# Expert tokens gathered in slots of 64 and two experts side by side in TensorE's array, in a two-layer trunk step

## The reference

```python
hf = rms_norm(x, p['norm_ffn_w']) * (1.0 + sc_f) + sh_f
x = x + g_f * hier_moe(hf, p)

def hier_moe(h, p):
    ...
    gw, gsel = lax.top_k(gp, 1)
    ...
    tw, ti = lax.top_k(jax.nn.softmax(el, axis=-1), TOP_K)
    tw = tw / jnp.sum(tw, axis=-1, keepdims=True)
    eid = gsel * EXPERTS_PER_GROUP + ti
    combine = jnp.sum(jax.nn.one_hot(eid, N_EXPERTS, dtype=jnp.float32) * (gw * tw)[..., None], axis=1)
    hg = jnp.einsum('nd,edf->nef', x, p['moe_w_gate'])
    hu = jnp.einsum('nd,edf->nef', x, p['moe_w_up'])
    act = jax.nn.silu(hg) * hu * combine.astype(x.dtype)[..., None]
    y = jnp.einsum('nef,efd->nd', act, p['moe_w_down'])
```

## Time and profile before

| | |
|---|---|
| median of 3 runs | 1421.93 us |
| span of the profiled execution | 1411.4 us |
| between the span and the median | 10.5 us |
| PE (matmul) busy | 1236.9 us, 88% |
| PEld (weight load) busy | 968.0 us, 69% |
| VectorE (DVE) busy | 678.2 us, 48% |
| ScalarE (ACT) busy | 491.7 us, 35% |
| GpSimd (POOL) busy | 86.5 us, 6% |
| DMA | 299.0 MB, mean 212 GB/s |
| expert loads | 64 of 3072 KB, median 10.1 us from issue to landing |

### The profile page before, as it was taken

How to read it: one execution, slowest core, us unless ns; L and a number is a source line. 1 busy time by engine, 2 the same in 40 slices (tenths; PEclk the granted TensorE clock), 3 DMA queues, 4 the chain that set the end, 5 groups by cost and what they waited for, 6 DMA issues and landing times.

```text
span 1411.4 us, 18228 instructions
## 1 busy us (share of the span) xinstructions
PE 1236.9 (88%) x7508; PEld 968.0 (69%) x7508; DVE 678.2 (48%) x857; ACT 491.7 (35%) x550; POOL 86.5 (6%) x93
## 2 busy tenths in 40 slices
PE   4689678998679999999967996798886999999997
PEld 3489568797656666666664985687776666666665
DVE  0255535443355556656423654445424556566652
ACT  2234521112244444444213444111322544444440
POOL 0000203130000000000000011222100000000000
PEclk8799879999789999999988997899996999999999
DMA  9744600121508888888865354102060488888960
GB/s 389 337 179 179 242 9 31 35 90 44 225 0 336 338 338 339 346 345 336 343 269 244 146 199 172 34 31 94 1 243 26 179 345 335 335 340 344 354 268 32
DMA packets 15195, 299.00 MB, mean 212 GB/s; under 512 B 1920, under 2 KB 1920, under 8 KB 2176
## 3 DMA queue, kind: packets, MB, share of 16 engines
q1 hardware_dynamic: 14688, 296.67, 53.5%
q0 software_dynamic: 416, 1.05, 0.2%
HBM read 295.61 MB, written 2.10 MB: 211 GB/s over the span
## 4 chain that ended last, share of the span: by engine, by line
PE 79%; DVE 6%; issue 5%; ACT 5%; DMA 3%; POOL 1%; SPq 0%; DVEq 0%; POOLq 0%; ACTq 0%
PE ps L824 16%; PE ps L795 8%; PE ps L796 8%; PE ps L797 8%; PE ps L713 4%; PE ps L483 3%; PE ps L485 3%; PE ps L484 3%; PE ps L663 3%; PE ps L638 3%; PE ps L659 3%; DMA param<-in_param 3%; PE ps L459 2%; PE ps L838 1%; PE ps L862 1%
## 5 line engine op out<-in xcount | busy, mean ns | idle before, releaser
L1602 DVE TENSOR_TENSOR ring_r<-ring,arena_r 128x2048 fp32r<-128x2048 f32 x124 | 284.3, 2292 | 129.5 <-ACT arena_r L1127 129.5
L1127 ACT ACTIVATE arena_r<-ring 128x2048 fp32r<-128x2048 f32 x124 | 236.7, 1909 | 231.2 <-PE ps L797 231.2
L795 PE MATMUL ps<-arena_r 128*128 128x512 f32 x512 | 231.3, 452 | 5.4 <-DVE ring_r L1602 3.5
L824 PE MATMUL ps<-ring,arena 128*128 128x512 f32 x512 | 230.3, 592 | 1.0 <-DVE arena L1608 1.0
L797 PE MATMUL ps<-ring_r,arena_r 128*128 128x512 f32 x512 | 202.5, 395 | 0.0
L796 PE MATMUL ps<-arena_r 128*128 128x512 f32 x512 | 202.3, 395 | 0.0
L824 PEld LDWEIGHTS ps<-ring,arena 128*128 128x128 f32 x512 | 96.8, 189 | 99.0 <-issue 91.9
L795 PEld LDWEIGHTS ps<-arena_r 128*128 128x128 f32 x512 | 96.3, 188 | 38.9 <-issue 16.7
L483 PE MATMUL ps<-arena_r 128*128 128x256 f32 x384 | 109.7, 286 | 10.4 <-DVE ring_r L1256 10.4
L796 PEld LDWEIGHTS ps<-arena_r 128*128 128x128 f32 x512 | 96.6, 189 | 31.8 <-issue 14.4
L797 PEld LDWEIGHTS ps<-ring_r,arena_r 128*128 128x128 f32 x512 | 96.0, 188 | 22.6
(11 more groups left out here) (301 smaller groups left out, 1548.9 us busy)
## 6 DMA issues: line engine op xcount, KB each, us to landing
ring<-in_moe SPq DMA_DIRECT2D x64, 3072.0 KB, 10.1
ring<-in_ada_w SPq DMA_DIRECT2D x16, 3072.0 KB, 11.1
ring<-in_w_feat SPq DMA_DIRECT2D x8, 3072.0 KB, 14.1
ring<-in_w_tok SPq DMA_DIRECT2D x2, 2112.0 KB, 24.0
ring<-in_w_out SPq DMA_DIRECT2D x2, 2048.0 KB, 7.3
ring<-in_w_out SPq DMA_DIRECT2D x4, 1024.0 KB, 4.9
param<-in_param SPq DMA_DIRECT2D x2, 1501.5 KB, 23.4
const<-in_const SPq DMA_DIRECT2D x1, 1899.0 KB, 16.6
```

The source lines that it names most:

```text
L795: mm(out, x_hi, hi[:, k], start=k == 0, stop=False)
L824: done = mm(bank(4 + half), act_t[:, i % 2, kk * P:(kk + 1) * P], ring[i % RING][:, at:at + 512], start=i == 0 and kk == 0, stop=i == PER_ ...
L1127: go(w_hi[:, 0:4096].rearrange("p (w n) -> p w n", w=2)[:, :, cols], ring[j][:, 0:4096].rearrange("p (w n) -> p w n", w=2)[:, :, cols], AC ...
L1602: tt(low_w, raw_w, high_w, ALU.subtract).then_inc(sem[name], 1)
```

## The change

The gather becomes one by expert, with 64 slots (`CAP`) for each, and the experts are worked in 16 pairs.

- Path: the condition is now `fullest < CAP + 1`, no expert with more than 64 tokens. The rank of a token is counted per expert instead of per group (`mask32`, five products of 32 columns instead of 4).
- Selection (`select`): an equality with the slot number, 8 experts x 64 slots = 512 columns, for one group at a time, in two buffers.
- Gather: for one group at a time, again 8 x 4 products of 512 columns. Group 0 is gathered ahead; of the next group two feature tiles are gathered in each pair. The gathered tokens `xg` are plain float32, copied alternately by ScalarE and VectorE, not split.
- Gate/up (L816) and down (L863): full precision, weights not split, so L1127, L1602 and their waits are gone from this path. The first expert of a pair takes columns 0 to 63 of the array (and PSUM partitions 0 to 63), the second columns 64 to 127, by `tile_position`; the instructions of the two alternate. Gate/up of a pair is 16 products of 512 columns, down 8.
- The slot weights are made pair by pair (four products of 2 columns, L807), the `sel` transposes too (two per pair, L849, beside the two of the activations, L851).
- After every pair its 128 rows are written out as high and low part and scattered (L827, 16 products of 256 columns), summed in PSUM banks 4 to 7 over all pairs. The residual comes after the last, all 16 instructions in one go.
- Loads: two transfers per expert, gate/up (2048 KB, waits for `up_mm`, the gate/up products of four experts earlier) and down (1024 KB, waits for `down_mm`).
- The first expert's split, which stood beside the output projection, moves into the dense path.

```diff
+CAP = HD
+PAIRS, TURN = N_EXPERTS // 2, PER_GROUP // 2
+GU_W = 4096
...
-                for e in range(RING):
-                    slot_free(l, HEAD_SLOTS - RING + e)
-                    ring_in(e, (src["moe"][l, e], SLOT))
-                with sp.Fori(1, N_EXPERTS // RING) as turn:
...
+                for q in range(PAIRS):
+                    for half in range(2):
+                        for e in (2 * q, 2 * q + 1):
+                            if e < RING:
+                                if half == 0:
+                                    slot_free(l, HEAD_SLOTS - RING + e)
+                            else:
+                                name = "down_mm" if half else "up_mm"
+                                sp.wait_ge(sem[name], rise(l, name, e - RING + 1))
+                            if half == 0:
+                                sp.dma_start(ring[e % RING][:, 0:GU_W], src["moe"][l, e][:, 0:GU_W]).then_inc(slot_in[e % RING], 16)
+                            else:
+                                sp.dma_start(ring[e % RING][:, GU_W:SLOT], src["moe"][l, e][:, GU_W:SLOT]).then_inc(down_in[e % RING], 16)
...
+                def gate_up(q):
...
+                    for k in range(KT):
+                        for i in range(2):
+                            last = mm(ps[64 * i:64 * i + 64, q % 2, :].rearrange("p (w n) -> p w n", w=2),
+                                      xg[:, g % 2, k, c0 + 64 * i:c0 + 64 * i + 64], weights[i][:, k],
+                                      start=k == 0, stop=k == KT - 1, tile_position=(0, 64 * i), skip_group_check=True)
+                    last.then_inc(sem["up_mm"], 2)
...
+                def pair_step(q):
...
+                    gate_up(q)
+                    if q > 0:
+                        scatter(q - 1)
+                    if g < N_GROUPS - 1:
+                        pe.wait_ge(sem["sel"], rise(l, "sel", g + 2))
+                        for n in range(2):
+                            gather(g + 1, 2 * turn + n, 2 + n)
+                    pe.wait_ge(sem["g_act"], rise(l, "g_act", q + 1))
+                    for s in range(NS):
+                        nc.tensor.transpose(ps[:, q % 2, TOK + s * P:TOK + (s + 1) * P], sel[:, g % 2, s, c0:c0 + P], ident)
+                    for kk in range(2):
+                        last = nc.tensor.transpose(ps[:, q % 2, kk * P:(kk + 1) * P], gat[:, q % 2, kk * P:(kk + 1) * P], ident)
+                    last.then_inc(sem["tr_mm"], 1)
...
+                    pe.wait_ge(sem["act_t"], rise(l, "act_t", q + 1))
...
+                    for half in range(2):
                         for kk in range(2):
...
+                                last = mm(ps[64 * i:64 * i + 64, 2 + half, :], act_t[:, q % 2, kk * P + 64 * i:kk * P + 64 * i + 64],
+                                          ring[(2 * q + i) % RING][:, at:at + 512], start=kk == 0, stop=kk == 1,
+                                          tile_position=(0, 64 * i), skip_group_check=True)
+                    last.then_inc(sem["down_mm"], 2)
+                    if q < PAIRS - 1:
+                        pe.wait_ge(sem["st_dve"], rise(l, "st_dve", q + 1))
+                        slot_weights(q + 1, q % 2)
```

More of the change, by code:

```diff
@@ L785, in step @@
                         down(e, j, last)
[L787 to L809, removed]
-                        for kk in range(2):
[L811 to L826, removed]
@@ new lines, in landed, with gather @@
+                def landed(arrived, e, per_layer, before):
+                    j = e % RING
+                    pe.wait_ge(arrived[j], l * (16 * per_layer) + 16 * (before + e // RING + 1))
+                def gather(g, k, bank_out):
+                    for n, (x, s) in enumerate((x, s) for s in range(NS) for x in (ht_hi, ht_lo)):
+                        last = mm(bank(bank_out), x[:, s, k * P:(k + 1) * P], sel_r[:, g % 2, s, :], start=n == 0, stop=n == 3)
+                    last.then_inc(sem["ga_mm"], 1)
@@ new lines, in scatter @@
+                def scatter(q):
+                    pe.wait_ge(sem["y_lo"], rise(l, "y_lo", q + 1))
+                    pe.wait_ge(sem["st_dve"], rise(l, "st_dve", q + 1))
+                    for f in range(KT):
+                        for y in (y_hi, y_lo):
+                            last = mm(ps[:, 4 + f // 2, (f % 2) * TOK:(f % 2 + 1) * TOK], y[:, f * P:(f + 1) * P], sel_t[:, q % 2, :],
+                                      start=q == 0 and f % 2 == 0 and y is y_hi, stop=q == PAIRS - 1 and y is y_lo, skip_group_check=True)
+                    last.then_inc(sem["scatter_mm"], 1)
@@ L866, in _ @@
-                    for name, n in (("cb_mm", 16), ("gate_mm", 32), ("up_mm", 32)):
+                            name = "ga_dve" if k % 2 else "ga_act"
+                            pe.wait_ge(sem[name], rise(l, name, (k - 4) // 2 + 1))
+                        gather(0, k, k % 4)
+                    pe.wait_ge(sem["c_lo"], rise(l, "c_lo", 1))
+                    slot_weights(0, 7)
+                    for q in range(PAIRS):
+                        pair_step(q)
+                    scatter(PAIRS - 1)
@@ L867, in _ @@
+                    for name, n in (("cb_mm", 16), ("gate_mm", 32)):
                         pe.sem_inc(sem[name], n)
@@ L1475, in _, with residual @@
                 tt(hT[:, 0:2, :].rearrange("p m t -> p (m t)"), gn, zg, ALU.mult).then_inc(sem["gn_out"], 1)
-                def residual(gate, tiles):
+                def residual(gate, tiles, bank0=0):
                     for f in tiles:
```

279 lines of the change are left out of this document (134 added, 145 removed).

## The result

| | before | after |
|---|---|---|
| median | 1421.53 us (1420.16 to 1423.93, 4 runs) | 1307.28 us (1306.3 to 1311.93, 4 runs) |
| ratio | | 0.921, 95% interval 0.918 to 0.924 |
| span of the profiled execution | 1411.4 us | 1305.4 us |

The change is faster by 7.9%. The forecast was 1309.0 us, between 1291 and 1345.

The account below looks back on a forecast made before the run. The prediction took TensorE to bound the kernel. Savings of 51.1 (pairs), 2.9 (entry) and 2.4 us (exit) per layer, 112.8 for both, cut the span from 1411.4 to 1298.6; adding 10.5 gave 1309 us, range 1291 to 1345.

Parts of the forecast that it names:

- What bounds it: While the experts run, TensorE sets the pace, busy 100%; taking away the weight split gains nothing by itself.
- Two tiles at 2.0 times: In gate/up and down, two column tiles run side by side at 2.0 times, with the products issued interleaved.
- The terms of a pair: TensorE's pieces for two experts sum to 16.12 us, or 14.04 without a gather; 51.1 us less per layer.
- The first pair: First two experts of a layer: no scatter covers the silu and its table load, so 14.93 us.
- Entry and exit: Gather start to first expert product 10.5 us, 2.9 less; last down projection to layer end 10.5 us, 2.4 less.
- Next layer: Change to layer two: adaLN loads and parameters come later, about 9.5 us after layer end; zero, up to 3 us lost.
- DMA: Expert weight loads: 6.29 MB per pair take 15.0 us at 420 GB/s, so DMA does not set the pace.
- the rival: Among the experts, DMA sets the pace below 381 GB/s; 1355 us at 346 GB/s, 1337 at 358; chance 0.20.
- The sum: Both layers: 56.4 us less each, 112.8 in all; span 1298.6 us, plus 10.5 from span to median, 1309 us.

Follow-up runs that it names:

- e3: The changed kernel with half the columns of every expert transfer, so half the bytes: 1306.97 us.
- e4: The changed kernel with the scatter moved behind the transposes and expert transfers of half the columns: 1286.46 us in one execution.
- e8: The changed kernel with scatter and slot-weight products moved before the down projection, and expert transfers of half the columns: 1274.51 us in one execution.
- e1: The changed kernel with one tile's products all issued before the other's instead of alternating: 1478.3 us in one execution.
- e7: The changed kernel with the scatter behind the transposes and the slot-weight products moved between scatter and down projection: 1272.32 us, ratio to before 0.897.
- e2: The changed kernel with the scatter of the pair before moved into the wait before the down projection: 1281.09 us, ratio to before 0.904.
- e0: The kernel before, unchanged, run again with each execution's time beside its span: 1420.29 us, median of ten executions.
- e5: The changed kernel with one 3 MB transfer per expert, waiting for the down projection four experts earlier: 1343.75 us, ratio to before 0.948.

## Why the prediction was right, and where it was not

**What bounds it.** Right: TensorE did and does (e3; with pairs shorter still, e4 and e8). No run removes the split alone. e1 has it removed, without the tiles' concurrency, and is slower than before.

**Two tiles at 2.0 times.** Right: 7.02 us for 16 products, 32 passes. At 0.43 us each they would take 13.7 one after the other, so 1.96 times, entry included, and 2.0 times without it (6.87 in e7). The section "Measured speedup vs the span model" of "TensorE: Matmul & The Clock Gate" in the Trainium skill gives 2.38 times for three column tiles of 32 columns, 79% of the ideal; two tiles of 64 columns in full precision lose much less here. The earlier trace rows pointed the right way, but their 3.7 of 4 would be 1.85 of 2: the prediction took the full 2.0 without a reason, and it held. What the prediction took over without weighing it was the interleaved order: e1 shows that without it the change is a loss.

**The terms of a pair.** All within 0.3 us, nearly all forecast too low:

| | forecast | after |
|---|---|---|
| gate/up | 6.96 | 7.02 |
| scatter | 1.84 | 2.11 |
| gather | 1.86 | 1.87 |
| transposes and copies | 1.47 | 1.32 |
| down | 3.53 | 3.65 |
| slot weights | 0.46 | 0.54 |
| sum | 16.12 | 16.51 |

(1.32 is the mean of two kinds of pair: 16.51 less the other terms.) The term that was missing is the way out of the tiles. I priced an entry and not an exit, so the scatter was put down at 16 x 0.115 though it stands right behind gate/up. e2 shows it as 0.2 us wherever the first full-width product stands, and e7 on the slot weights (0.54 against 0.34), so a pair pays it twice. In the slot weights it was hidden by a price too high, 0.46 for 0.34. The section "Key Properties" of "TensorEngine Tiling (Array Packing)" in the Trainium skill says that changing the tiling drains the engine. The trace agrees that a change costs time, and puts 0.15 us on the way in and 0.2 on the way out. Together the pairs took 253.25 us instead of 248.0: of the 51.1 us forecast per layer, 45.8 came.

**The first pair.** 14.77 us against 14.93. The table load that was to lengthen it starts at 401.49 us, as the gather ends, and is over before gate/up begins.

**Entry and exit.** Entry 11.14 us against 10.5, exit 9.54 against 10.5. In the entry the last of the gather's products starts 9.67 us after the first, not 9.5, and the way from there over the last copy to the first product takes 1.47 us, not 1.0. The prediction also misread how the gather starts: 11 of its 32 products in the kernel before, and 12 in the change, go 0.43 us apart, and not half; the sum used the measured 9.5 us and did not suffer. In the exit the scatter was priced at 3.3 us, as in the earlier trace rows, where the granted clock from 707.7 to 711.0 us was 0.60. It took 2.82, with 0.72 granted; why the clock rose sooner no run shows. The residual took 4.22 of the 4.5.

**Next layer.** The parameters came 14.0 us after the layer's end, later than the 9.5 forecast, but the output projection of layer two starts 301.8 us after that end, where it was 301.1. Zero, with 0.7 us lost, lay within the 3 us allowed; e0, the kernel before again, took 305.9 us for the same way, so 0.7 is not clear of its spread. The timeline of after:

```profile
679.62 0.69 DVE L1211 TENSOR_TENSOR param<-param,const 128x512 f32<-128x512 f32 x1 [14.00 <-DMA param<-in_param]
```

**DMA.** The forecast expected about 390 GB/s and had the rival begin below 381. Measured are 384, which is about what pairs of 16.51 us ask for (6.29 MB in that time are 381 GB/s), and that was no wall: e7 draws 416. The rival's price (1337 to 1355 us) has its likeness in e5, where the same bytes ask late; what it got wrong is the cause. The section "Where 436 GB/s comes from" of "DMA: Bandwidth & Descriptors" in the Trainium skill has the memory bind a core at about 358 GB/s, half of what two cores share. Here one core loads, and the trace differs: 384 GB/s in the change, 416 in e7.

**The sum.** In layer one 51.5 us came instead of 56.4. Layer two, from its gather to the end of the span, gave 53.6; ahead of the first gather 1.2 us were gained and between the layers 0.3 lost. Span against span that is 1411.4 − 1305.4 = 106.0 us instead of 112.8. The forecast of 1309 still fell within 2 us of the median, and there luck has a part. The step "the median of the runs, 1421.93, lies 10.5 us above that span" took the distance for something fixed around the span. The runs show 1.6 to 1.9 us around every span. So the profiled execution of before was in all likelihood a short one, some 1413 us, of a kernel that varies from 1410.02 to 1423.93 us; its own total is not on record. Had I used 1.8, the forecast would have been 1300.4, 7 us low. The sum was 7 us too hopeful and the offset 9 us too high. Seen by the medians, 114 us were gained and 113 forecast: some 8 us of the gain lie outside the two profiled spans, and the prediction had no term for them. The granted clock of 0.92 or 1.00 ahead of the output projection (e0) is worth 3 us of such a difference; the rest stays open.

## What to carry to other kernels

Full-precision products with 64 stationary columns go two for the time of one when they alternate between column tiles; let the order of issue change tile at least every two products (which cost the down projection 0.02 us), keep the tiled stretches together, and count 0.35 us for each time in and out. Look next at the pause for the copied transposes, which half of gate/up used to cover: moving independent work there was worth 26 us (e2), and joining the two tiled stretches of a pair another 9 (e7). Prove or rule out a DMA bound by halving the bytes, since shares of 0.95 and even 1.00 were no sign of one here; and ask for a slot's pieces when each piece comes free, which with the smaller transfers was worth 36 us.

## What was unexpected of the hardware

- A tile's products overlap the other tile's without alternating, for four passes: gate/up takes 7.02, 8.90 and 12.22 us in blocks of one, four and eight products, and down loses 0.02 us in blocks of two.
- Leaving the tiles costs 0.2 us on whatever comes first (scatter 2.11 against 1.91, gather 2.06 against 1.87, slot weights 0.54 against 0.34).
- In e7 one core drew 416 GB/s of loads in windows of 50 us, at a share of 1.00, without its TensorE being late.
- The spread of the kernel before, 1410 to 1424 us, is larger than the 0.3% by which I meant to tell a change. The period of 9.24 us among the experts was equal in its two profiles; part of the spread is the clock granted ahead of the output projection, 0.92 or 1.00, which makes one stretch of the same products 52.3 or 49.4 us long.
